# The delta rule's chunk matrices kept as 64 columns per chunk, each product as two 64-row tiles, in a two-block transformer kernel on one core

## What is computed

```
decay = jnp.cumsum(g, axis=-1)
l_mask = jnp.where(tril, jnp.exp(jnp.where(tril, diff, 0.0)), 0.0)
a_strict = jnp.where(strict, jnp.einsum('bhnid,bhnjd->bhnij', k_beta, k) * l_mask, 0.0)
t_mat = a_strict + jnp.eye(CHUNK, dtype=f32)
value = lax.linalg.triangular_solve(t_mat, v_beta, ...)
k_cumdecay = lax.linalg.triangular_solve(t_mat, k_beta * jnp.exp(decay)[..., None], ...)
attn_intra = jnp.where(tril, jnp.einsum('bhnid,bhnjd->bhnij', q, k) * l_mask, 0.0)
...
v_new = val - jnp.einsum('bhcd,bhde->bhce', kc, S)
o = jnp.einsum('bhcd,bhde->bhce', qd, S) + jnp.einsum('bhij,bhje->bhie', att, v_new)
S = S * cd[..., None, None] + jnp.einsum('bhcd,bhce->bhde', kt, v_new)
```

## Time and profile before

| | |
|---|---|
| median of 3 runs | 1162.4 us (1162.31 to 1166.04) |
| the profiled execution: span from the first to the last instruction | 1160.9 us |
| what the fastest two runs have beyond that span | 1.4 to 1.5 us |
| PE busy in the span | 1130.3 us, 97% |
| PE's mean granted clock | 0.992 of full speed |
| the part of the program that the change touches | 64 to 156 us of the span |

### The profile page before, as it was taken

The page is one execution under the profiler, slowest core; times in us unless marked ns, Lnnn a source line. Parts: engine busy times, 40 slices in busy tenths (PEclk is TensorE's granted clock), DMA queues, the critical chain, the costliest instruction groups (busy, mean ns, idle before and its releaser), DMA issues.

```text
span 1160.9 us, 18111 instructions
## 1 busy us (share of the span) xinstructions
PE 1130.3 (97%) x7361; PEld 865.5 (75%) x7361; DVE 613.5 (53%) x885; ACT 515.0 (44%) x849; POOL 196.0 (17%) x132
## 2 busy tenths in 40 slices
PE   8999999999799899999999999999999999999996
PEld 7988878999688788878888886666666666666664
DVE  6989767789864696596466643222222222222223
ACT  6666353744465374854655433223222233222223
POOL 1339860124442331400000000000000000000000
PEclk9999999999899899999999999999999999999999
DMA  9952642576556666565366479999999999999994
GB/s 322 286 184 73 227 145 97 197 286 225 213 216 233 203 198 193 187 218 174 133 201 260 175 264 418 425 421 421 425 423 422 427 422 422 427 422 422 424 423 185
DMA packets 82698, 332.01 MB, mean 286 GB/s; under 512 B 4555, under 2 KB 6926, under 8 KB 66110
## 3 DMA queue, kind: packets, MB, share of 16 engines
q1 hardware_dynamic: 81236, 328.43, 73.0%
q0 software_dynamic: 1088, 2.34, 1.0%
q10 hardware_dynamic: 298, 0.11, 0.0%
HBM read 329.83 MB, written 1.05 MB: 285 GB/s over the span
## 4 chain that ended last, share of the span: by engine, by line
PE 81%; DMA 7%; DVE 6%; POOL 3%; ACT 2%; issue 1%; DVEq 0%; SPq 0%; ACTq 0%; POOLq 0%
PE bank L1087 17%; PE bank L441 12%; PE bank L442 12%; PE bank L443 12%; PE bank L1106 9%; PE bank L1077 5%; DMA ring<-in_w_exp_down 3%; POOL ring L2644 3%; DMA ring<-in_w_ada 2%; PE bank L568 2%; DVE ring_r L1820 2%; PE bank L1134 1%; PE bank L1135 1%; ACT ring L1398 1%; PE bank L1094 1%
## 5 line engine op out<-in xcount | busy, mean ns | idle before, releaser
L1820 DVE TENSOR_TENSOR ring_r<-ring,arena_r 128x2048 fp32r<-128x2048 f32 x93 | 224.6, 2424 | 130.8 <-ACT arena_r L1307 129.2
L1307 ACT ACTIVATE arena_r<-ring 128x2048 fp32r<-128x2048 f32 x93 | 177.2, 1916 | 148.7 <-PE bank L443 66.8
L2644 POOL TENSOR_TENSOR ring<-ring 128x512 f32<-128x512 f32 x84 | 149.0, 1797 | 234.6 <-ACT ring L1398 205.6
L443 PE MATMUL bank<-arena_r,actT_r 128*128 128x512 f32 x384 | 150.5, 392 | 0.0
L441 PE MATMUL bank<-arena_r,tok_r 128*128 128x512 f32 x352 | 140.9, 400 | 1.7 <-DVE con L2285 1.7
L442 PE MATMUL bank<-ring_r,tok_r 128*128 128x512 f32 x352 | 138.2, 393 | 0.0
L2457 DVE TENSOR_TENSOR arena<-bank,arena 64x512 f32<-64x512 f32 x62 | 42.7, 689 | 175.4 <-PE bank L1106 174.7
L441 PE MATMUL bank<-tok_r,arena_r 128*128 128x256 f32 x352 | 99.5, 283 | 1.8 <-DVE actT_r L1837 1.2
L443 PE MATMUL bank<-tok_r,ring_r 128*128 128x256 f32 x352 | 98.3, 279 | 0.0
L442 PE MATMUL bank<-actT_r,arena_r 128*128 128x256 f32 x352 | 98.2, 279 | 0.0
L2443 DVE TENSOR_TENSOR arena<-bank,arena 128x256 f32<-128x256 f32 x32 | 13.6, 425 | 149.8 <-ACT arena L1739 93.8
(11 more groups left out here) (424 smaller groups left out, 1830.3 us busy)
## 6 DMA issues: line engine op xcount, KB each, us to landing
ring<-in_w_in SPq DMA_DIRECT2D x22, 2048.0 KB, 9.3
ring<-in_w_exp_down SPq DMA_DIRECT2D x22, 2048.0 KB, 21.3
ring<-in_w_exp_gate SPq DMA_DIRECT2D x21, 2048.0 KB, 22.0
arena<-in_w_exp_up SPq DMA_DIRECT2D x21, 2048.0 KB, 23.5
ring<-in_w_ff SPq DMA_DIRECT2D x16, 2048.0 KB, 8.7
ring<-in_w_ada SPq DMA_DIRECT2D x12, 2048.0 KB, 11.2
arena<-in_w_exp_gate SPq DMA_DIRECT2D x11, 2048.0 KB, 21.6
arena<-in_w_exp_down SPq DMA_DIRECT2D x10, 2048.0 KB, 21.5
```

The lines of the kernel that those rows point to most:

```text
L443: return mm(o, l[1], r[0], start=False, stop=stop)
L1307: A(hi, w, ACT.Copy).then_inc(S["w_high"], 1)
L1820: TT(half(i, ringR)[0], w, hi.bitcast(fp32), ALU.subtract).then_inc(S["w_rest"], 1)
L2644: i = nc.gpsimd.tensor_tensor(w[:, k, :], w[:, k, :], w[:, k + n, :], ALU.add)
```

## The change

Each chunk matrix is kept in 64 columns instead of 128. Tile t's four heads then take 256 columns, and the two chunks of a tile lie above each other, on partitions 0 to 63 and 64 to 127, in the same columns. Each product of two 128 by 128 matrices becomes two products of 64 by 64 matrices, whose operands and results lie on the two halves of the partitions. All DVE and ACT steps on these matrices (ET, AT, MT, DI, DT, YY) are 256 instead of 512 columns wide for one tile. D0 is a matmul with an identity instead of a transpose. kc, whose result is 128 rows high, takes two banks for a tile, one for each chunk, with 64 contracted rows each, and so two copies on ACT instead of one. R is made with the block constant "blk" as weights, 256 columns wide. The constants keep their total size ("spare" fills it up), so their DMA is as before. The core of the diff (the other lines are the same change of widths from 512 to 256):

```diff
--- before.py
+++ after.py
@@ constants
-    put("negT", np.where(same & (row <= col), 0.0, NEG))
+    inrowC, incolC = row % C, col[:, :C]
+    put("cumC", inrowC <= incolC)
+    put("identC", inrowC == incolC)
+    put("negC", np.where(inrowC <= incolC, 0.0, NEG))
...
+    put("spare", np.zeros((P, 7 * P - 9 * C)))
@@ program
-        ET, DI, DT, YY, AT, MT = ar(15360, 1024), DQ, DK, QD, kbT, qT
-        VAL, KC, VN = KB, QD, ET
+        ET, DI, DT, YY, AT, MT = [x[:, 0:8 * C] for x in (ar(15360, 1024), DQ, DK, QD, kbT, qT)]
+        VAL, KC, VN = KB, QD, ar(15360, 1024)
@@ tensor engine
-                end(mm(bk[:, :], ones, YY[:, t * 512:(t + 1) * 512], start=True, stop=True), f"R{t}")
+                end(mm(bk[:, 0:256], K("blk"), YY[:, t * 256:(t + 1) * 256], start=True, stop=True), f"R{t}")
-            def product(name, dst, lhs, rhs, t):
+            def chunk_products(name, t, out_at, lhs_at, rhs_at):
                 bk = begin(f"{name}{t}")
                 for h in range(DH):
-                    o = (4 * t + h) * P
-                    i = mm(bk[:, h * P:(h + 1) * P], lhs[:, o:o + P], rhs[:, o:o + P], start=True, stop=True)
+                    for r in (0, C):
+                        i = mm(out_at(bk, h, r), lhs_at(4 * t + h, r), rhs_at(4 * t + h, r), start=True, stop=True)
                 end(i, f"{name}{t}")
+            def within(a):
+                return lambda n, r: a[r:r + C, n * C:(n + 1) * C]
+            def block_rows(a):
+                return lambda n, r: a[r:r + C, n * P:(n + 1) * P]
+            def block_cols(a):
+                return lambda n, r: a[:, n * P + r:n * P + r + C]
+            def product(name, lhs, rhs, t):
+                chunk_products(name, t, lambda bk, h, r: bk[r:r + C, h * C:(h + 1) * C], within(lhs), within(rhs))
...
-                        product(f"kk{x}", None, kT, rhs, t)
+                        chunk_products(f"kk{x}", t, lambda bk, h, r: bk[r:r + C, h * C:(h + 1) * C], block_cols(kT),
+                                       block_cols(rhs))
...
-                    i = nc.tensor.transpose(bk[:, h * P:(h + 1) * P], DT[:, o:o + P], ident)
+                    for r in (0, C):
+                        i = mm(bk[r:r + C, h * C:(h + 1) * C], within(DT)(4 * t + h, r), K("identC")[r:r + C, :],
+                               start=True, stop=True)
...
-                product("val", None, DT, DV, t)
-                product("kc", None, KBE, DT, t)
+                chunk_products("val", t, lambda bk, h, r: bk[r:r + C, h * P:(h + 1) * P], within(DT), block_rows(DV))
+                for r in (0, C):
+                    bk = begin(f"kc{t}_{r}")
+                    for h in range(DH):
+                        i = mm(bk[:, h * C:(h + 1) * C], block_rows(KBE)(4 * t + h, r), within(DT)(4 * t + h, r),
+                               start=True, stop=True)
+                    end(i, f"kc{t}_{r}")
@@ scalar engine
-                bk = wait_full(act, f"kc{t}")
-                done(copy(KC[:, t * 512:(t + 1) * 512], bk[:, :]), f"kc{t}")
+                for r in (0, C):
+                    bk = wait_full(act, f"kc{t}_{r}")
+                    done(copy(v3(KC[:, t * 512:(t + 1) * 512], DH)[:, :, r:r + C], v3(bk[:, 0:256], DH)), f"kc{t}_{r}")
@@ vector engine
-                TT(v3(YY, 8), bm(K("cumT"), 8), bc(gl, P), ALU.mult).then_inc(S["cumg"], 1)
+                TT(v3(YY, 8), bm(K("cumC"), 8), bc(gl, C), ALU.mult).then_inc(S["cumg"], 1)
...
-                done(TT(v3(YY[:, o], 4), v3(bk[:, :], 4), bm(K(f"lvl{LEVELS[l]}"), 4), ALU.mult), f"Y{l}{t}")
+                done(TT(v3(YY[:, o], 4), v3(bk[:, 0:256], 4), bm(K(f"lvl{LEVELS[l]}"), 4), ALU.mult), f"Y{l}{t}")
```

More of the change, by code:

```diff
@@ L51, in constants @@
     put("blk", same)
-    put("negT", np.where(same & (row <= col), 0.0, NEG))
+    inrowC, incolC = row % C, col[:, :C]
+    put("cumC", inrowC <= incolC)
+    put("identC", inrowC == incolC)
+    put("negC", np.where(inrowC <= incolC, 0.0, NEG))
+    lower, upper = np.minimum(inrowC, incolC), np.maximum(inrowC, incolC)
     for s in [1] + LEVELS:
-        m = (col // (2 * s) == row // (2 * s)) & ((col // s) % 2 == 1) & ((row // s) % 2 == 0)
-        put(f"lvl{s}", -1.0 * (m if s == 1 else m.T))
+        m = (upper // (2 * s) == lower // (2 * s)) & ((upper // s) % 2 == 1) & ((lower // s) % 2 == 0)
+        put(f"lvl{s}", -1.0 * (m & ((inrowC < incolC) if s == 1 else (inrowC > incolC))))
+    put("spare", np.zeros((P, 7 * P - 9 * C)))
     put("causT", np.where(row <= col, 0.0, NEG))
@@ L664, in _ @@
                     wait_read(pe, f"D0{t}" if l == 0 else f"Dn{l - 1}{t}")
-                    product(f"Y{l}", None, AT, DI, t)
+                    product(f"Y{l}", AT, DI, t)
                     if t == 0:
@@ L672, in _ @@
                     if not last:
-                        product(f"Dn{l}", None, DT, YY, t)
-                    product(f"Dt{l}", None, YY, DT, t)
+                        product(f"Dn{l}", DT, YY, t)
+                    product(f"Dt{l}", YY, DT, t)
             for t in range(T):
@@ L696, in _ @@
                         for x in (0, 1):
-                            wait_read(pe, f"kc{x}")
+                            for half_of in (0, C):
+                                wait_read(pe, f"kc{x}_{half_of}")
                             wait_read(pe, f"dT3{x}")
@@ L1390, in _ @@
                 act.wait_ge(S["et_req"], t + 1)
-                A(ET[:, t * 512:(t + 1) * 512], ET[:, t * 512:(t + 1) * 512], ACT.Exp).then_inc(S["et_exp"], 1)
+                A(ET[:, t * 256:(t + 1) * 256], ET[:, t * 256:(t + 1) * 256], ACT.Exp).then_inc(S["et_exp"], 1)
             def ada_scaled(c):
@@ L1417, in _ @@
                 bk = wait_full(act, f"D0{t}")
-                done(copy(DI[:, t * 512:(t + 1) * 512], bk[:, :]), f"D0{t}")
+                done(copy(DI[:, t * 256:(t + 1) * 256], bk[:, 0:256]), f"D0{t}")
             ada_scaled(1)
@@ L1882, in decays @@
                     bk = wait_full(dve, f"R{t}")
-                    e = v3(ET[:, t * 512:(t + 1) * 512], 4)
-                    done(TT(e, v3(bk[:, :], 4), bc(dec[:, 4 * t:4 * t + 4], P), ALU.subtract), f"R{t}")
+                    e = v3(ET[:, t * 256:(t + 1) * 256], 4)
+                    done(TT(e, v3(bk[:, 0:256], 4), bc(dec[:, 4 * t:4 * t + 4], C), ALU.subtract), f"R{t}")
                     wait_read(dve, f"R{t}")
-                    TT(e, e, bm(K("negT"), 4), ALU.add).then_inc(S["et_req"], 1)
+                    TT(e, e, bm(K("negC"), 4), ALU.add).then_inc(S["et_req"], 1)
             def head_sums(x):
@@ L1955, in _ @@
                     bk = wait_full(dve, f"kk{x}{t}")
-                    o = slice(t * 512, (t + 1) * 512)
-                    done(TT(dst[:, o], bk[:, :], ET[:, o], ALU.mult), f"kk{x}{t}")
+                    o = slice(t * 256, (t + 1) * 256)
+                    done(TT(dst[:, o], bk[:, 0:256], ET[:, o], ALU.mult), f"kk{x}{t}")
                     wait_read(dve, f"kk{x}{t}")
@@ L1967, in masked @@
                 bk = wait_full(dve, f"Y{l}{t}")
[L1968 to L1969 removed]
+                o = slice(t * 256, (t + 1) * 256)
+                done(TT(v3(YY[:, o], 4), v3(bk[:, 0:256], 4), bm(K(f"lvl{LEVELS[l]}"), 4), ALU.mult), f"Y{l}{t}")
             def corrected(l, t):
[L1972 removed]
+                o = slice(t * 256, (t + 1) * 256)
                 if l < len(LEVELS) - 1:
                     bk = wait_full(dve, f"Dn{l}{t}")
[L1975 removed]
+                    done(TT(DI[:, o], bk[:, 0:256], DI[:, o], ALU.add), f"Dn{l}{t}")
                 bk = wait_full(dve, f"Dt{l}{t}")
[L1977 removed]
+                done(TT(DT[:, o], bk[:, 0:256], DT[:, o], ALU.add), f"Dt{l}{t}")
             def mod_cols(c):
```

6 lines of the change are left out of this document (3 added, 3 removed).

## The result

The changed kernel takes 1148.6 us (median of four runs, 1147.5 to 1149.7) where the kernel before takes 1162.4: ratio 0.9877, 95% interval 0.986 to 0.9895. It is faster, and by 13.8 us, where 8.2 were forecast.

What follows compares the result with a forecast made beforehand. PE, busy 97% of the span, was taken as the bound, with DVE already late at three places. Nine items along PE's path summed to -8.15 us, from 1162.4 to 1154 us, range 1150.5 to 1160.5.

Steps and rivals of the forecast that it cites:

- The product (0.46): Each 128 by 128 product, as 16 records on two row tiles side by side, takes 0.46 us instead of 0.886.
- no overlap: Rival: two row tiles writing one bank do not overlap, 0.86 us a product, 1163.4 us in all; chance 0.08.
- emptying the array at each switch: Rival: each change between the two tiles costs 0.15 us, a product 2.05, 1192 us in all; chance 0.05.
- the floor of 0.04 to 0.05 a record: Rival: small records cannot go below 0.04 to 0.05 us, adding 4 to 8 us, 1160 us in all; chance 0.10.
- R: Item 1, ahead of kk: four records of half the width save 0.9 us.
- kk and the first Y: Items 2 and 3, ahead of level 0: kk saves 1.4 us, D0 and the first Y save 0.5.
- Level 0: Item 4, up to Y of level 1: DVE's list sets the time afterwards; saves 1.9 us.
- Level 1: Item 5, to Dn of tile 1: DVE sets it, only two masks shrink, saves 0.55 us; PE's wait grows to 2.2.
- items 6 (+0.6) and 7 (+0.5): From 120.86 to first scores, and level 3: late DVE masks cost these amounts; the items still save 2.8 and 1.8 us.
- Items 8 and 9: Level 4 until the first val saves 0.7 us; val and kc, kc taken without overlap, cost 2.4 more.
- a shift of PE carries them along: Behind 156 us, weight transfers and POOL's sums are released by PE's own steps, so they move with PE.
- a rival that could only grow them: Gain lost to POOL or a load: PE waits, later POOL waits could grow, -3 us instead of -8, 1159; chance 0.05.

## Why the prediction was wrong

Direction and mechanism held; the time lies below the range. Point by point:

**The product (0.46).** Measured 0.47. The Trainium skill, "TensorEngine Tiling (Array Packing)", section "Restrictions and Gotchas", Gotcha 1, has it that different row tiles can't access one bank at once. The trace disagrees: 448 records on two row tiles of one bank, in different partitions, took 15.0 us, 0.033 each with all ends, and 0.043 with the tiles in turn. The rivals of no overlap and of emptying the array at each switch fall with that, and the floor of 0.04 to 0.05 a record too.

**The mis-sized terms** make 1.65 together. R gave about 0.5 less: its records took 0.96 as forecast, but it started 0.6 later than before, behind ACT's table load, which began at 60.86 where it had begun at 59.95. That is ahead of all that was changed, so this piece is a difference between two executions and no error of the term. kk and the first Y held (the Y was done 2.3 earlier where 2.8 were summed, R's miss). Level 0 gave 0.5 less. Level 1 gave 1.0 and not 0.55, and PE's wait behind KBE was 1.6 and not 2.2, since DVE's KBE step, 1.90 before, took 1.45. The late masks of items 6 (+0.6) and 7 (+0.5) did not come: no wait stands before 120.03 or in the block at 128.68. Items 8 and 9, summed at +1.7, cost 0.7 (10.5 to 9.8): the sixteen kc records of a tile, two banks, took 1.53 with the change of shape, where the sum had 1.76 and the change apart. At 0.096 a record, and 0.065 when the two chunks alternate, the forecast's "nothing overlaps" was too strict; where the overlap lies no run shows.

By these alone the time would be 1162.4 - 9.8 = 1152.6, inside the range.

**The step that failed** is the one behind the sum: "a shift of PE carries them along". It took all that follows 156 us as one rigid piece, and left the shift's effect on the later waits to a rival that could only grow them. The kernel before paid for a wait of 2.9 us in its tenth turn and for half clock behind it, and both hang on one near miss: a transfer that landed 1.0 late put POOL's last step 0.25 us behind a DVE step in place of ahead of it. The run with the tenth turn moved measures it at 3.7 of the 13.8 us, net of what the move costs; the runs with 1.1 and 2.2 us of work added, at 4.4 and 4.8. They also show that work added does away with it as well as time saved. The earlier trace rows had both that wait and its half clock in them. The price was there to be read, 2.9 + 15 x 0.23 = 6.4 at most; missing was the question whether the wait survives a shift. These 4 us are luck: the change removed the wait only by shifting what lies behind it.

## What to carry to other kernels

Small float32 matmuls gain by narrower weights and by two row tiles whose instructions alternate, also into one PSUM bank with different partitions: put the tile's loop innermost. Where a change moves everything behind it, look at each later wait and ask by how much its two sides missed each other; a wait made by a DVE step that starts a fraction of a microsecond ahead of a POOL step can go with any shift, and a kernel before that contains one flatters the change. To learn how much of a difference is of that kind, delay the old kernel by a few different amounts, a microsecond or two each, and time it.

## What the hardware showed that was not expected

- Work added made a kernel faster: 10 transposes, 1.1 us, took 3.3 us off (1163.0 to 1159.7).
- A POOL addition of 128x512 takes 1.3 us alone and 3.2 to 3.4 when a DVE step on two SBUF operands starts just ahead of it; started first, it isn't lengthened and DVE is (5.10 for two steps, 4.49 alone).
- A record with 128 columns of weights costs 0.113 us for 64 moving columns as for 128; with 64 columns of weights on alternating row tiles 0.029 to 0.031; with 128 columns of weights on 64 rows, alternating, 1.04/16 = 0.065.
- With two waits of 1.51 and 1.55 us, their ends 2.2 us apart, the granted clock was at 0.50 by the end of the second; with waits of 0.95, 0.63 and 1.60 us within 5 us it stayed at 1.00.
